# The opening of the first attention: panel splits ahead of late tokens, keys by chunk, and the bias store in another place

## The chip, the core and the metric

One core of one Trainium2 chip runs the kernel. Times are device microseconds of one execution; the kernel before took 1206.1 us as the median of three runs (1205.81 to 1208.53). Its engines are TensorE (PE), VectorE (DVE), ScalarE (ACT), GpSimd (POOL) and SyncE (SP), which here only issues DMA transfers. SP and ACT have a DMA queue each (q1 and q10 in the profile).

## What is computed

A two-layer block (differential attention, then multi-scale pooling, each with a SwiGLU feed-forward) feeds a second block with three sparse attentions and another feed-forward, all in float32 on 256 tokens of width 1024. The change touches the first attention and one store for the second block:

```python
# adaLN: six vectors of 1024 per layer, for the tokens and for the context
m = jax.nn.silu(cond) @ w_mod + b_mod            # split into 6 components
hx = x * (1 + scale) + shift                      # components 0 and 1
hc = context * (1 + c_scale) + c_shift
q = rope(hx @ w_q); k = concat(hc @ w_k, rope(hx @ w_k)); v = concat(hc @ w_v, hx @ w_v)
p = softmax(q_m k_m^T / 8) for m in (0, 1)        # 8 heads, two maps each
o = (p_0 - lam * p_1) v;  o = rms(o) * g;  y = o @ w_o
x = layer_norm(alpha * x + g1 * y)                # g1 is component 2
# second block: 28 relative-bias heads, a row of 384 values each, spread to (28, 128, 384)
```

## The kernel before

**Panels.** All weights pass through a ring of four slots of 1 MB (`ring0` to `ring3`), in the fixed order of `w_panels`. For the attention that is panels 0 to 11: keys of heads 0 to 3 over the first half of the width (0), queries (1), the same keys over the second half (2), queries (3), values of four heads (4, 5), keys of heads 4 to 7 (6, 7), queries (8, 9), values (10, 11). Each panel is split into a high part (`w_hi`, written by ACT, two buffers) and a low part (`ring_lo`, the difference, written by DVE); TensorE computes each product as three matmuls, high x high, high x low, low x high (`product`). ACT may write a high part only when the panel two before is used, SP may load a slot only when the panel four before is used. On ACT and DVE `split_to(i)` writes all parts up to panel i that are still missing, at that place of the engine's own order.

**Tokens.** TensorE turns tokens and context into `whole` by eight chunks of 128 columns. The first four are scaled from PSUM (`high_tokens`, `low_tokens`); the other four wait for the second half of components 0 and 1 and are scaled later. Each of these four raises `late_tokens` by one.

**Components.** Four 2 MB pieces of `w_mod` are multiplied on TensorE (`mod_rows_first`, `mod_columns_first`). The others come in halves m = 0, 1, 2, ... of 2 MB: DVE sums a half in four steps over 1024 columns (`mod_product(m)`), the last step raises `mod_acc`; when both halves of a component are in, TensorE adds over partitions (`mod_sums(comp)`, two banks of the pool "misc", banks 6 and 7) and DVE adds the bias (`mod_finish(comp)`). SP loads half m when `mod_acc` has reached m - 1. Half m has its place in SP's order ahead of a panel: 0 before panel 4, 1 before 5, 2 before 6, 3 before 7, 4 and 5 before 10, 6 before 11, 7 before 12.

**Scores.** Units u = 0 to 7 are four heads by two query tiles. TensorE makes two score maps per unit in the pool "score" (banks 4 to 7: even units 4 and 5, odd units 6 and 7), DVE takes their extrema (`maxima`), ACT the exponentials (`exps`), DVE the mix (`combine`, raises `probs_done`). Between them `maxima_and_mixes` and `scores_out` do panel splits. TensorE then turns the probabilities (pool "misc") and multiplies the values.

**Order.** Every engine runs in program order, and the order of each is written out by hand, in the functions printed below; waits on semaphores alone tie them together. The bias store (`scratch` from `srow`, 28 x 128 rows of 384 values) is issued by ACT at line 1341. SP loads it back as `bias` ahead of panel ("ffn1_in", 6, 1), at line 2682, and waits for `srow_stored` first.

## Time and profile before

| | us |
|---|---|
| median of the runs | 1206.1 |
| the profiled execution | 1208.5 |
| its span, first to last instruction | 1206.7 |
| TensorE busy | 1119.9 |
| DVE busy | 786.0 |
| ACT busy | 491.6 |

The profile is of one execution. A row of a timeline gives the start, the duration, engine, line, operation, the tiles written and read, and in brackets how long the engine had stood idle and what released it. The granted clock is the share of TensorE's full 2.4 GHz; the mean over the span is 0.965. Lines of the kernel stand as L1261. L622 is the one line that issues every matmul, so a matmul is told by its tiles. The shares of the DMA engines are rough near 1.

### The profile page before, as it was taken

Reading aid. Unit: us, or ns where it says so; the run is one execution under the profiler, and the core shown is the slowest. Engines: PE = TensorE matmul, PEld = TensorE weight load, DVE = VectorE, ACT = ScalarE, POOL = GpSimd, SP = SyncE. Lnnn points to the kernel's source line nnn. Section 1 sums busy time; section 2 is a strip of 40 time slices with the busy share of each in tenths; the row PEclk is TensorE's granted clock in tenths of the full one; section 3 lists DMA queues with packets and bytes.
Section 4 is the critical chain, followed back from the end, with each engine's and each line's share of the span. In section 5 each row is a group of like instructions: output and inputs, shape, how many; then the busy total and the mean of one; then the engine's idle time right before and its main releaser. Section 6 shows DMA issues by size and latency. Waiting matters only on the chain.

```text
span 1206.7 us, 17048 instructions
## 1 busy us (share of the span) xinstructions
PE 1119.9 (93%) x7015; PEld 969.1 (80%) x7015; DVE 786.0 (65%) x1073; ACT 491.6 (41%) x625; POOL 99.8 (8%) x84
## 2 busy tenths in 40 slices
PE   4878999979999999599999989999999988999998
PEld 2665786759999877499998878887777767999987
DVE  2376867768878878777554485569873685555543
ACT  2242433534333332433333365465655534434332
POOL 0000000000000001000000000244656000000000
PEclk9788999899999998899999989999999998999999
DMA  9695462483997787257755536534333343555552
GB/s 337 244 378 210 166 253 70 143 310 115 360 330 275 263 300 257 88 172 258 251 175 196 179 115 202 164 116 140 106 116 129 120 159 121 192 177 177 185 198 105
DMA packets 145135, 236.98 MB, mean 196 GB/s; under 512 B 4901, under 2 KB 86306, under 8 KB 144930
## 3 DMA queue, kind: packets, MB, share of 16 engines
q1 hardware_dynamic: 138128, 221.12, 54.1%
q10 hardware_dynamic: 6930, 14.77, 3.3%
q8 instruction: 56, 0.92, 0.3%
q14 instruction: 21, 0.17, 0.0%
HBM read 229.32 MB, written 6.55 MB: 195 GB/s over the span
## 4 chain that ended last, share of the span: by engine, by line
PE 80%; DVE 9%; ACT 4%; issue 4%; DMA 1%; ACTq 1%; POOL 1%; DVEq 0%; SPq 0%
PE bank L622 77%; PE bank L697 3%; ACT w_hi L1261 2%; DVE ring_lo L1661 2%; DMA ring<-in_ffn_w_out 1%; ACTq L1293 1%; DVE modacc L1782 1%; DVE y_tok L1972 1%; DVE small L1974 1%; POOL ring_lo L2604 1%; DVE y_tok L1970 0%; DMA big<-in_ln_b 0%; DVE small L1861 0%; ACT hc_hi L1321 0%; DVE tmp L1845 0%
## 5 line engine op out<-in xcount | busy, mean ns | idle before, releaser
L1661 DVE TENSOR_TENSOR ring_lo<-ring,w_hi 128x2048 fp32r<-128x2048 f32 (+3 forms) x145 | 325.4, 2245 | 274.4 <-ACT w_hi L1261 274.1
L1261 ACT ACTIVATE w_hi<-ring 128x2048 fp32r<-128x2048 f32 (+3 forms) x157 | 295.0, 1880 | 445.9 <-PE bank L622 412.4
L622 PE MATMUL bank<-h_hi,w_hi 128*128 128x256 f32 x1056 | 302.9, 287 | 5.6 <-DVE h_lo L1680 3.3
L622 PE MATMUL bank<-h_lo,w_hi 128*128 128x256 f32 x1056 | 300.6, 285 | 0.0
L622 PE MATMUL bank<-h_hi,ring_lo 128*128 128x256 f32 x1056 | 300.5, 285 | 0.0
L622 PEld LDWEIGHTS bank<-h_hi,w_hi 128*128 128x128 f32 x1056 | 204.6, 194 | 7.4 <-DVE h_lo L1680 3.9
L622 PEld LDWEIGHTS bank<-h_lo,w_hi 128*128 128x128 f32 x1056 | 204.7, 194 | 1.0 <-issue 1.0
L622 PEld LDWEIGHTS bank<-h_hi,ring_lo 128*128 128x128 f32 x1056 | 204.5, 194 | 0.0
L622 PE MATMUL bank<-w_hi,h_hi 128*128 128x512 f32 (+4 forms) x320 | 127.2, 398 | 11.1 <-DVE h_lo L1908 7.8
L622 PE MATMUL bank<-w_hi,h_lo 128*128 128x512 f32 (+4 forms) x320 | 123.7, 387 | 0.0
L622 PE MATMUL bank<-ring_lo,h_hi 128*128 128x512 f32 (+4 forms) x320 | 123.6, 386 | 0.0
L622 PE MATMUL bank<-w_hi,ff_hi 128*128 128x512 f32 x264 | 103.0, 390 | 1.4 <-DVE ring_lo L1661 1.0
L622 PE MATMUL bank<-ring_lo,ff_hi 128*128 128x512 f32 x264 | 102.8, 389 | 0.0
L622 PE MATMUL bank<-w_hi,ff_lo 128*128 128x512 f32 x264 | 102.7, 389 | 0.0
L1782 DVE SCALAR_TENSOR_TENSOR modacc<-aux,cs,modacc 128x1024 f32<-128x1024 f32 x70 | 89.8, 1283 | 1.5
L622 PEld LDWEIGHTS bank<-w_hi,h_hi 128*128 128x128 f32 x320 | 62.0, 194 | 25.0 <-DVE h_lo L1908 8.8
L2614 POOL TENSOR_TENSOR small<-small,neghalf 128x1 f32<-128x1 f32 (+2 forms) x16 | 12.9, 803 | 791.5 <-DVE small L1984 450.8
L622 PEld LDWEIGHTS bank<-w_hi,h_lo 128*128 128x128 f32 x320 | 61.7, 193 | 11.3
L622 PEld LDWEIGHTS bank<-ring_lo,h_hi 128*128 128x128 f32 x320 | 62.1, 194 | 10.0
L2604 POOL TENSOR_TENSOR ring_lo<-ring,w_hi 128x512 fp32r<-128x512 f32 x48 | 61.5, 1313 | 49.2 <-ACT w_hi L1261 49.2
L622 PE MATMUL bank<-big 64*128 64x128 f32 (+5 forms) x274 | 55.8, 448 | 6.0 <-issue 1.6
L622 PEld LDWEIGHTS bank<-w_hi,ff_hi 128*128 128x128 f32 x264 | 49.6, 188 | 13.1 <-issue 3.0
(269 smaller groups left out, 1446.5 us busy)
## 6 DMA issues: line engine op xcount, KB each, us to landing
aux<-in_w_mod SPq DMA_DIRECT2D x24, 2048.0 KB, 10.1
ring<-in_ffn_w_in SPq DMA_DIRECT2D x88, 512.0 KB, 4.9
ring<-in_w_in SPq DMA_DIRECT2D x24, 1024.0 KB, 5.0
ring<-in_ffn_w_out SPq DMA_DIRECT2D x22, 1024.0 KB, 5.3
ring<-in_w_ffn_in SPq DMA_DIRECT2D x44, 512.0 KB, 4.6
ring<-in_attn_w_qkv SPq DMA_DIRECT2D x12, 1024.0 KB, 13.3
ring<-in_w_ffn_out SPq DMA_DIRECT2D x11, 1024.0 KB, 5.0
bias_rows<-srow ACTq DMA_DIRECT2D x1, 5376.0 KB
```

Of the source, the lines that this page charges most:

```text
L622: return nc.tensor.matmul(o, l, r, start=start, stop=stop, **kw)
L697: ins = nc.tensor.transpose(bank[0:src.shape[1], i * P:i * P + src.shape[0]], src, ident[0:src.shape[0], 0:src.shape[0]])
L1261: nc.scalar.activation(panel_part(i, 0), raw_panel(i), ACT.Copy).then_inc(w_hi, 1)
L1293: act.dma_start(dst, src).then_inc(cols_landed, 16)
L1661: V.tensor_tensor(panel_part(i, 1), raw_panel(i), panel_part(i, 0).bitcast(F32), ALU.subtract)\
L1782: ins = V.scalar_tensor_tensor(modacc_raw[:, :], w[:, j, :], c, modacc_raw[:, :], ALU.mult, ALU.add)
L1972: step(V.scalar_tensor_tensor(y, x_tok[:, tt, sl], ALPHA, y, ALU.mult, ALU.add))
L1974: step(V.bn_stats(small[:, 100 + 12 * tt + 6 * nb:106 + 12 * tt + 6 * nb], y))
L2604: ins = nc.gpsimd.tensor_tensor(panel_part(i, 1)[:, c, :], raw_panel(i)[:, c, :], panel_part(i, 0)[:, c, :].bitcast(F32), ALU.subtract)
L2614: nc.gpsimd.tensor_tensor(dst, src, exponent, ALU.pow).then_inc(rstd_done, 1)
```

## The change

Six things move; no instruction is added or taken away.

1. ACT and DVE split panel 0 before the early token chunks, and panel 2 (with panel 1) before the late ones.
2. The keys of panel 2 run chunk by chunk over all four heads (`late_keys`), each chunk behind its own `late_tokens`, instead of head by head.
3. TensorE's `mod_sums(2)` goes from between the value tiles to behind the last scores; `mod_sums(3)` and `mod_sums(4)` go later.
4. DVE's `mod_product(1)` goes from in front of the rotary steps to between units 2 to 5 of the scores, `mod_product(2)` from there to behind them; `mod_product(4)`, `mod_finish(2)` and `mod_finish(4)` go later.
5. DVE's split of panel 5 goes behind both rotary pairs.
6. ACT issues the bias store in the second feed-forward ("ffn1", block 1) instead of behind the late token chunks.

```diff
 # TensorE
-                for c in range(PK):
-                    if h == 0 and kg == 1:
-                        pe.wait_ge(late_tokens, c + 1)
...
+            def late_keys():
+                key = ("qkv", 2, 1)
+                w = panel(key)
+                for c in range(PK):
+                    pe.wait_ge(late_tokens, c + 1)
+                    for h in range(4):
+                        ins = product(psum[where[("K", h)][0]], [x[:, c, h * P:(h + 1) * P] for x in w],
+                                      [x[:, PK + c, :] for x in hcT], False, c == PK - 1)
+                        if c == PK - 1:
+                            fills(ins, ("K", h))
+                release(key, ins, ("K", 3))
...
                 queries(0, 0, late_columns)
-                for j in range(4):
-                    keys(0, 1, j)
+                late_keys()
                 queries(0, 1)
...
-                    if i == 3:
+                    if i == 5:
                         mod_sums(3)
...
-                mod_sums(4)
                 swap_keys(2)
                 swap_keys(3)
                 queries(1, 1)
+                mod_sums(4)
...
-                if hg == 0:
-                    mod_sums(2)
                 vals(hg, 0, 1)
...
                 for u in (6, 7):
                     scores(8 * hg + u)
+                if hg == 0:
+                    mod_sums(2)
 # ACT
+            split_to(0)
             for n in (0, 1):
                 wait_emptied(act, ("modcol", n))
...
-            split_to(1)
+            split_to(2)
...
-            act.wait_ge(srow_done, 1)
-            act.dma_start(scratch, srow[:, :].unsqueeze(1).broadcast_to([REL_HEADS, P, SROW])).then_inc(srow_stored, 16)
...
+                    if name == "ffn1" and nb == 1:
+                        act.wait_ge(srow_done, 1)
+                        act.dma_start(scratch, srow[:, :].unsqueeze(1).broadcast_to([REL_HEADS, P, SROW]))\
+                            .then_inc(srow_stored, 16)
 # DVE
+            split_to(0)
             for ch in range(PK):
                 low_tokens(ch)
...
-            split_to(1)
+            split_to(2)
...
-            def maxima_and_mixes(hg):
+            def maxima_and_mixes(hg, m):
...
                     if 2 <= u <= 5:
-                        mod_product((2, 6)[hg], [u - 2])
+                        mod_product(m, [u - 2])
...
-            split_to(2)
+            split_to(3)
             mod_product(0)
-            split_to(3)
-            mod_product(1)
             split_to(4)
             turn_pair("K", 0)
             turn_pair("K", 1)
-            split_to(5)
             turn_pair("Q", 0)
             turn_pair("Q", 1)
+            split_to(5)
+            maxima_and_mixes(0, 1)
             mod_finish(2)
-            maxima_and_mixes(0)
+            mod_product(2)
             mod_product(3)
             split_to(8)
             mod_finish(3)
-            mod_product(4)
             head_var(0)
             head_norm(0)
+            mod_product(4)
+            split_to(9)
             mod_product(5)
             split_to(10)
-            mod_finish(4)
...
             head_norm(1)
+            mod_finish(4)
...
-            maxima_and_mixes(1)
+            maxima_and_mixes(1, 6)
```

DVE between `mod_product(0)` and the first scores, as the kernel before has it. L1661 is the low part of a panel (the number is its ring slot), L1777 and L1782 are `mod_product`, L1845 to L1849 the rotary steps, L1800 is `mod_finish(2)`, L1861 a `maxima`:

```order
L1777 TENSOR_SCALAR modacc<-aux,cs 128x1024
L1782 SCALAR_TENSOR_TENSOR modacc<-aux,cs,modacc 128x1024 x3
L1661 TENSOR_TENSOR ring_lo3<-ring3,w_hi1 128x2048
L1782 SCALAR_TENSOR_TENSOR modacc<-aux,cs,modacc 128x1024 x4
L1661 TENSOR_TENSOR ring_lo0<-ring0,w_hi0 128x2048
...
L1849 TENSOR_TENSOR big<-big,tmp 128x2x256
L1661 TENSOR_TENSOR ring_lo1<-ring1,w_hi1 128x2048
...
L1800 SCALAR_TENSOR_TENSOR aux<-bank,aux 128x512 x2
L1861 TENSOR_REDUCE small<-bank 128x2 x2
```

And the same stretch now, to the first `mod_product` step between the scores (lines are 12 or 13 higher: L1673 low part, L1858 to L1862 rotary steps, L1794 `mod_product`, L1874 `maxima`):

```order
L1794 SCALAR_TENSOR_TENSOR modacc<-aux,cs,modacc 128x1024 x3
L1673 TENSOR_TENSOR ring_lo0<-ring0,w_hi0 128x2048
L1858 TENSOR_TENSOR tmp<-bank,big 128x512
...
L1862 TENSOR_TENSOR big<-big,tmp 128x512
L1673 TENSOR_TENSOR ring_lo1<-ring1,w_hi1 128x2048
L1874 TENSOR_REDUCE small<-bank 128x2 x2
...
L1887 SCALAR_TENSOR_TENSOR aux<-tmp,small,aux 128x512
L1794 SCALAR_TENSOR_TENSOR modacc<-aux,cs,modacc 128x1024
```

The four L1782 of `mod_product(1)` behind `ring_lo3` have gone down among the scores, one to a unit, and the low part of ring slot 1 stands behind the rotary steps.

SP's order is the same in both kernels; with its waits it reads, from half m2 on:

```order
L480 DMA aux<-in_w_mod 128x4x1024 [waits mod_acc]
L2688 DMA ring2<-in_attn_w_qkv 128x4x512 [waits bank_filled3]
L480 DMA aux<-in_w_mod 128x4x1024 [waits mod_acc]
L2688 DMA ring3<-in_attn_w_qkv 128x4x512 [waits bank_filled5]
L2688 DMA ring0<-in_attn_w_qkv 128x4x512 [waits w_used]
```

These are m2, panel 6, m3, panel 7 and panel 8. Nothing moved, but the second `mod_acc` wait is now for sums that DVE makes among the scores.

TensorE at the end of the scores of units 6 and 7, before (`big` are the scores, `hc_hi,w_hi0` the keys of panel 6) and now:

```order
L622 MATMUL bank<-big 128x512 x4
L622 MATMUL bank<-hc_hi,w_hi0 128x512
```

```order
L622 MATMUL bank<-big 128x512 x4
L622 MATMUL bank<-modacc,ones 128x512 x2
L622 MATMUL bank<-hc_hi,w_hi0 128x512
```

The two matmuls of `mod_sums(2)` stand between the last scores and the next keys.

## Rows read from the trace of the kernel before

**Rows 1.** The page of the kernel before, part 1: busy time of each engine.

```profile
PE 1119.9 (93%) x7015; PEld 969.1 (80%) x7015; DVE 786.0 (65%) x1073; ACT 491.6 (41%) x625; POOL 99.8 (8%) x84
```

**Rows 2.** Timeline of TensorE: start us, us, engine, line, op, tiles, xcount, [idle before].

```profile
38.14 0.77 PE L622 MATMUL bank<-hc_hi,w_hi 128*128 128x512 f32 x1 [3.07 <-DVE ring_lo L1661]
...
69.91 0.77 PE L622 MATMUL bank<-hc_hi,w_hi 128*128 128x512 f32 x1 [6.67 <-DVE ring_lo L1661]
...
97.25 1.10 PE L622 MATMUL bank<-modacc,ones 128*128 128x512 f32 x2 [2.09 <-DVE tmp L1845]
99.28 1.22 PE L622 MATMUL bank<-modacc,ones 128*128 128x512 f32 x1 [0.93 <-DVE tmp L1845]
...
130.15 1.99 PE L622 MATMUL bank<-big 64*128 64x512 f32 x8
...
137.64 1.03 PE L697 MATMUL bank<-table,aux 128*128 128x128 f32 x8
```

**Rows 3.** One stretch: us, PE busy, granted clock, DMA share, GB/s.

```profile
98.00:105.00 7.00, 6.07 (x13) 0.53 0.85 325
```

**Rows 4.** Timeline of DVE: last late chunk, low part 2, end of mod_product(2).

```profile
66.91 0.69 DVE L1833 TENSOR_TENSOR hc_lo<-big,hc_hi 128x512 fp32r<-128x512 f32 x1
67.52 2.29 DVE L1661 TENSOR_TENSOR ring_lo<-ring,w_hi 128x2048 fp32r<-128x2048 f32 x1
...
129.81 1.28 DVE L1782 SCALAR_TENSOR_TENSOR modacc<-aux,cs,modacc 128x1024 f32<-128x1024 f32 x1
```

**Rows 5.** Timeline of ACT: two key copies, w_hi of panels 6 and 7.

```profile
75.08 0.60 ACT L1344 ACTIVATE big<-bank 128x512 f32<-128x512 f32 x1 [6.74 <-PE bank L622]
77.82 0.60 ACT L1344 ACTIVATE big<-bank 128x512 f32<-128x512 f32 x1 [2.15 <-PE bank L622]
...
113.61 1.91 ACT L1261 ACTIVATE w_hi<-ring 128x2048 fp32r<-128x2048 f32 x1 [2.39 <-PE bank L622]
...
134.02 1.92 ACT L1261 ACTIVATE w_hi<-ring 128x2048 fp32r<-128x2048 f32 x1
```

**Rows 6.** DMA issues at 9.8 and 217 us: KB each, us to landing.

```profile
ring<-in_attn_w_qkv SPq DMA_DIRECT2D x1, 1024.0 KB, 16.7
...
aux<-in_w_mod SPq DMA_DIRECT2D x1, 2048.0 KB, 7.8
ring<-in_attn_w_o SPq DMA_DIRECT2D x1, 1024.0 KB, 10.4
```

**Rows 7.** Timeline of SP's queue: m3, and panel 7 with the two behind it.

```profile
83.67 1.41 SPq L480 DMA_DIRECT2D aux<-in_w_mod  x1
89.01 41.61 SPq L2675 DMA_DIRECT2D ring<-in_attn_w_qkv  x3
```

**Rows 8.** DMA queues, 60.9 to 105.5: packets, MB, share of 16 engines.

```profile
q1 hardware_dynamic: 3806, 10.94, 64.6%
q10 hardware_dynamic: 3593, 5.50, 32.9%
```

**Rows 9.** Two stretches, second feed-forward: busy by engine, clock, DMA share, GB/s.

```profile
535.50:562.80 27.30, 27.30 (x230) 27.30 (x230) 25.25 (x22) 9.65 (x7) 0.00 (x0) 1.00 0.65 219
562.80:584.00 21.20, 21.20 (x169) 20.24 (x168) 9.86 (x9) 7.23 (x6) 0.00 (x0) 1.00 1.07 342
```

**Rows 10.** Timeline of SP's queue: bias load, and the panel issues behind it.

```profile
562.82 0.43 SPq L2682 DMA_DIRECT2D aux<-bias_rows  x1
567.54 6.80 SPq L2675 DMA_DIRECT2D ring<-in_ffn_w_in  x2
```

**Rows 11.** Timeline of ACT, second feed-forward: splits and one issue of rows.

```profile
532.99 1.91 ACT L1261 ACTIVATE w_hi<-ring 128x2048 fp32r<-128x2048 f32 x1 [3.85 <-PE bank L622]
...
544.51 0.39 ACTq L1279 DMA_DIRECT2D aux<-in_ln_g  x1
...
581.99 1.91 ACT L1261 ACTIVATE w_hi<-ring 128x2048 fp32r<-128x2048 f32 x1 [5.06 <-DMA ring<-in_ffn_w_in]
...
586.53 1.92 ACT L1261 ACTIVATE w_hi<-ring 128x2048 fp32r<-128x2048 f32 x1 [2.14 <-PE bank L622]
```
## The prediction

> **What bounds the kernel now.** The page comes first: TensorE is busy 93% of the span [rows 1], so only what shortens or lengthens TensorE's own path counts. Its rows in order of time show where it stands still in the first attention: 3.07 us before the first key product, 6.67 us before the second key panel, until DVE has written that panel's low part, and 2.09 and 0.93 us at the sums of component 2, which wait for DVE's rotary steps [rows 2]. After such a pause the granted clock sits at half, the 1.2 GHz level: 0.53 as a mean from 98 to 105 [rows 3]. The first key tile of the second panel took from 69.91 to its copy at 75.08, 5.2 us, the next one 2.74 us [rows 2, 5]; so the pause of 6.67 us cost 2.4 us more. Then I read the queues behind the moved steps: DVE, ACT, SP, and the two DMA queues, here and in the second feed-forward, where the bias store goes.
>
> Panels are numbered by their place in the loading order: 0 and 2 are the first four key heads, 4 and 5 the values, 6 and 7 the other keys; m0 to m3 are the first 2 MB halves of w_mod.
>
> **Step 1, splits ahead of the tokens.** ACT's w_hi of panel 0 (1.9 us a panel) moves ahead of the four early token chunks. The panel is there: issued at 9.85, it took 16.7 us and landed at 26.6 [rows 6], about when ACT begins those chunks. The token chain slides 2 us, and the last transposes, which ended at 38.14 - 3.07 = 35.1, end at 37.1. Before, TensorE had to wait beyond them for the low part; now that is long done. The first product comes at 37.1 and not 38.14; at half clock about half of it stays: **0.6 us gained**. Panel 2 is now split before the late tokens. Its w_hi waits only until panel 0 is used, and its low part (2.29 us, rows 4) ends about 55.7 instead of standing in front of TensorE. The copies of the two w_mod sums now queue behind it on DVE, until 57.1; TensorE asks for them at 57.8, so that wait is hidden by 0.7 us.
>
> **Step 2, keys chunk by chunk.** The last late chunk is done at 67.5 [rows 4]; with the shift of 0.6 the four come at 62.8, 64.2, 65.6 and 66.9. One chunk for four heads is 12 products, 2.74 us. So TensorE waits for the first chunk alone, about 0.2 us, and never again: **6.5 us gained**, and with the clock kept **2.2 us**. The fourth key tile is full at 73.8, not 83.1, a lead of 9.3 us.
>
> **Step 3, the sums of component 2.** They leave their place between the value tiles. There they cost 2.09 + 0.93 us of waits and 1.10 us each, 5.2 us [rows 2], and the slow clock behind them, 6 us of products at half speed, 3.0 us [rows 3]. DVE now turns keys and queries with no low part between them and is ahead of TensorE. The lead when panel 4 is released and ACT begins panel 6 (113.61 before, rows 5) is 9.3 + 5.2 + 3.0, some **17.7 us**: 95.9.
>
> **Step 4, what this starts to wait for.** mod_product(1) moves in between the softmax steps, where mod_product(2) stood. Its last step, which ended there at 131.1 [rows 4], ends at 131.1 - 17.7 + 0.5 = 113.9 (a multiply-add of 1.28 us in the first place instead of 0.75). SP may issue m3 only when that sum is counted, and **panel 7 is queued behind m3 on SP**. Before, the two went out at 83.67 and 89.01 [rows 7]; now both at 114.0. A pair of the same sizes, issued 0.4 us apart, landed after 7.8 and 10.4 us [rows 6], so panel 7 lands at 124.8. ACT has its split between the last two exponentials (134.02 before, rows 5); it would come there at 116.4 and stands until 124.8. exps(7) follows at 126.7. TensorE is through with the scores (130.15 + 1.9 before) at 114.0 and now meets the sums of component 2, whose banks 6 and 7 are those of the last scores: exps(7) frees them at 127.4 and 128.1. TensorE idles 13.4 us, starts at 1.2 GHz, and the next keys begin at 129.2. With about 3 us of them slow, the probabilities of units 0 and 1 are turned at 136.4, against 137.64 [rows 2]. Of 17.7 us **1.2 stay**.
>
> **Step 5, the rest of the attention.** mod_sums(3) and (4) are the same instructions later; DVE does mod_finish, mod_product(4) and low part 9 in a new order. DVE then reaches the second rotary pair 2.3 us later, which the wait for low part 11 covers; query tile 3 is full 1.7 us earlier, but the value tile behind it needs TensorE as long as before. I count **0.4 us gained** (0 to 1.5). Opening in all: **-1.6 us**, between -4 (the clock recovers early, twice) and +0.5 (panel 7 lands 2 us later).
>
> **Step 6, the bias store in the second feed-forward.** The store takes 32.9% of the 16 DMA engines for 44.6 us, **14.7 us of all of them** [rows 8]. At its old place TensorE did not wait for the loads that it slowed. ACT now issues it right behind the split at 532.99 [rows 11]; its 0.93 us of issue are covered by ACT's idle time. From 535.5 to 562.8 the engines are 0.65 busy, and 1.07 is what they reach when full [rows 9]: 27.3 x 0.42 = 11.5 us are free. The store needs 14.7. At 562.82 SP wants to issue the load of the bias, which waits for the store, and the next panel is behind it [rows 10]. So SP stands for the last 3.2 us of the store, a share of the panel in flight and the landing, some 2 to 6 us; I take 4. That next panel was already the tightest: it went out at 567.54 behind the load, ACT waited 5.06 us for it until 581.99, and its two splits (1.9 and 2.3 us) ended at 586.2, where TensorE changed panels at about 586.5, as the next split shows [rows 10, 11]. So 0.3 us is left. A delay of 4 is a pause of 3.7 us on TensorE and, as above, some 2.4 us of slow clock: **+6.1 us**.
>
> There is a second way to the same price. ACT issues the normalisation rows at 544.51, now behind the store [rows 11]. On SP the issues behind the big bias load were held: 6.80 us for two [rows 10]. If ACT is held in the same way until the store is two thirds done, about 554.5, its next split starts at 555.6 instead of 550.3, the low part is ready at 559.9, and TensorE, which changes panels at 556.0, pauses 3.9 us: 6.3 with the clock. SP's delay is then absorbed, since TensorE comes later. The cost is **6 us by either way, 12 if both add up, 0 if neither holds**.
>
> The Trainium skill (DMA: Bandwidth & Descriptors, Queues, rings and completion order) says that each DMA engine takes turns between its queues packet by packet, so a store from ACT does not stand behind SP's panels but between them. In the stretch of the old store the rows agree: 3806 packets of one queue, 3593 of the other [rows 8]. By that rule alone each panel beside the store would land some 4 us later, within the two panels that it has, and the sum would stay as above.
>
> **Sum.** -1.6 + 6.0 = +4.4 us. The profiled execution had a span of 1206.7 us and a time of 1208.5, 2.4 above the median of 1206.1; on its own terms it becomes a span of 1211.1. Against the median I say **1210.5 us**.
>
> **Rivals.**
> A (forecast, 0.50): panel 7's late load swallows the opening's lead, and the store costs 3 to 8 us: 1207.5 to 1213.
> B (0.27), not slower: the store fits. The deciding point is 562.8: if the engines can give it 0.54 of those 27.3 us, nothing waits. For it: the engines reached 1.07 with other packets, and larger ones may run quicker. Against it: the free share as read is 0.42. Then only -1.6 is left, 1204.5, down to 1202 with the better end of the opening.
> C (0.10), clearly faster: the lead survives, because something I hold for fixed is not, such as panel 7 landing within 3 us of the sum, or TensorE having work across the wait. With 1.3 us of new waits and the store free, 1206.1 - 17.7 + 1.3 = 1189.7; with step 6, 1195.7. Against it: the pair in rows 6 took 10.4 us.
> D (0.13), worse: both ways of step 6 add up, or panel 7 lands late as well: +10, 1216.
>
> **How the numbers follow.** The measurement tells about 0.3%, 3.6 us. Slower by more than that: 0.38 of A's 0.50 and all of D, 0.51. Within it: 0.12 of A and 0.19 of B, 0.31. Faster: 0.08 of B and all of C, 0.18. The range may leave out 0.2: 1201.5 to 1216 leaves C and the far part of D.
>
> **What the new profile would show.** Right: the first product near 37, the second key panel near 63 with no pause; m3 and panel 7 issued together near 114; ACT waiting about 8 us for a ring landing, and TensorE pausing 13 us ahead of the component 2 sums; in the second feed-forward a bias load that SP issues several us late against its panel, or an ACT issue of the normalisation rows that takes many us, and a TensorE pause of 3 to 5 us with a half-clock stretch behind it. Wrong: the first probabilities turned before 130 (step 4), or a bias load that did not wait for the store (step 6).

## The result, and the profile after

| | before | after |
|---|---|---|
| median, us | 1205.95 (4 runs, 1204.85 to 1208.53) | 1215.37 (4 runs, 1214.24 to 1216.12) |
| ratio, 95% interval | | 1.0078 [1.0064, 1.0092] |
| span of the profiled execution | 1206.7 | 1213.9 |

The change makes the kernel 9.4 us slower; 1210.5 was predicted, in a range of 1201.5 to 1216. The direction and the first cause (the opening's gain is mostly swallowed by a late panel 7) came out as forecast. The store in the second feed-forward cost more than twice its term.

**The opening.** TensorE of after, in order of time (to compare with [rows 2]):

```profile
60.78 0.47 PE L622 MATMUL bank<-hc_hi,w_hi 128*128 128x512 f32 x1 [0.27 <-DVE hc_lo L1846]
...
111.32 1.99 PE L622 MATMUL bank<-big 64*128 64x512 f32 x8
125.57 2.04 PE L622 MATMUL bank<-modacc,ones 128*128 128x512 f32 x2 [12.26 <-ACT big L1374]
...
134.39 1.03 PE L697 MATMUL bank<-table,aux 128*128 128x128 f32 x8
```

The pause of 6.67 us before the second key panel is 0.27 us. The last scores are issued at 111.3 and not 130.2: 18.8 us ahead. Then TensorE stands 12.26 us in front of the sums of component 2, and of the lead 3.25 us is left when the first probabilities are turned (134.39 against 137.64). The chain behind that pause can be read backwards through ACT, DVE and SP:

```profile
113.85 0.69 ACT L1374 ACTIVATE big<-bank,small 128x512 f32<-128x512 f32 x1 [1.44 <-DVE small L1874]
...
122.85 1.91 ACT L1271 ACTIVATE w_hi<-ring 128x2048 fp32r<-128x2048 f32 x1 [7.55 <-DMA ring<-in_attn_w_qkv]
124.67 0.67 ACT L1374 ACTIVATE big<-bank,small 128x512 f32<-128x512 f32 x1
```

```profile
110.99 1.28 DVE L1794 SCALAR_TENSOR_TENSOR modacc<-aux,cs,modacc 128x1024 f32<-128x1024 f32 x1
```

```profile
112.29 0.37 SPq L480 DMA_DIRECT2D aux<-in_w_mod  x1
112.70 3.88 SPq L2688 DMA_DIRECT2D ring<-in_attn_w_qkv  x3
```

The last step of mod_product(1) on DVE ends at 112.27, SP issues m3 at 112.29 and panel 7 at 112.70. ACT is through with the exponentials of unit 6 at 115.3 and stands 7.55 us for panel 7, whose split lies ahead of the exponentials of unit 7. Those free the banks 6 and 7 that TensorE wants. Before, SP had both loads out by 89.0 [rows 7].

**The second feed-forward.** ACT's rows of after, to set beside [rows 11]:

```profile
528.70 1.91 ACT L1271 ACTIVATE w_hi<-ring 128x2048 fp32r<-128x2048 f32 x1 [3.85 <-PE bank L622]
528.71 0.93 ACTq L1473 DMA_DIRECT2D bias_rows<-srow  x1
...
540.22 1.92 ACT L1271 ACTIVATE w_hi<-ring 128x2048 fp32r<-128x2048 f32 x1 [3.84 <-PE bank L622]
540.23 13.51 ACTq L1289 DMA_DIRECT2D aux<-in_ln_g  x1
553.78 2.04 ACTq L1289 DMA_DIRECT2D aux<-in_ln_b  x1
555.92 0.60 ACT L1480 ACTIVATE tmp<-bank 128x512 f32<-128x512 f32 x1 [13.78 <-issue]
556.41 1.90 ACT L1271 ACTIVATE w_hi<-ring 128x2048 fp32r<-128x2048 f32 x1
```

An issue that took 0.39 us takes 13.51 us, with the store ahead of it in the same queue. ACT does nothing meanwhile ("13.78 <-issue"), and TensorE, out of split panels, stops:

```profile
563.28 0.55 PE L622 MATMUL bank<-h_hi,w_hi 128*128 128x256 f32 x1 [11.58 <-DVE ring_lo L1673]
```

Behind it 96 products take 14.26 us instead of 11.6, at half clock. The pause and the slow clock together are 14.2 us. The DMA engines in windows of after (columns as in [rows 9]):

```profile
540.00:550.00 10.00, 10.00 (x86) 10.00 (x85) 3.69 (x3) 1.92 (x1) 0.00 (x0) 1.00 0.96 271
550.00:560.00 10.00, 1.70 (x15) 1.50 (x13) 3.35 (x5) 2.44 (x3) 0.00 (x0) 0.77 1.01 297
560.00:570.00 10.00, 6.72 (x35) 6.75 (x36) 9.54 (x8) 2.35 (x2) 0.00 (x0) 0.55 0.93 295
```

They are full at 271 to 297 GB/s, while [rows 9] shows 342 GB/s when they are full of panels and the bias load. So two suspects stood in this stretch: ACT's held issue, and panels that land late beside the store. The experiments had to part them.

**Where the time stands, place by place.** ACT's split of a panel starts when TensorE has used the panel two before it, so the same split in two traces gives the lead or lag of the whole program. In us against before, negative is ahead; ordinary numbers are differences of two rows of ACT's timelines. The profiled execution of the kernel before (1208.53 us) is its slowest of the four, 2.6 us above the median, so a lead in this table can be that much too large:

| split at (before) | after | store back | m3 later | both | sums 2nd key |
|---|---|---|---|---|---|
| 64.6 (panel 2) | -15.4 | -15.4 | -15.6 | -17.9 | -15.7 |
| 113.6 (panel 6) | -19.4 | -19.4 | -19.5 | -21.9 | -19.7 |
| 147.4 (panel 8) | -3.2 | -3.0 | -11.0 | -12.9 | -16.6 |
| 267.9 | -4.7 | -4.4 | -12.2 | -13.9 | -15.8 |
| 538.8 | -4.3 | -3.9 | -12.6 | -13.3 | -15.2 |
| 567.6 | +10.0 | -3.9 | +0.7 | -13.3 | -15.2 |
| 975.0 | +9.9 | -4.0 | +1.6 | -13.0 | -15.1 |
| 1126.3 | +7.2 | -5.3 | +3.2 | -14.4 | -16.4 |

The columns are the kernel after and four of the experiments below. Between 975 and 1126 nothing differs in the code; some 1 to 3 us there, and the 2 us by which "both" is early at its first panels (its first keys had the full clock), are differences between single executions.

### The profile page after: what moved, and what is told of

The parts are those of the page before. It is cut to its first block, busy times and chain, and to the rows that moved or that the text cites. A ratio compares the mean times of both kernels' runs of the same rounds, so it can differ in the third digit from the quotient of the medians.

```text
span 1213.9 us, 17049 instructions
## 1 busy us (share of the span) xinstructions
PE 1112.8 (92%) x7015; PEld 964.8 (79%) x7015; DVE 785.9 (65%) x1073; ACT 491.9 (41%) x625; POOL 101.8 (8%) x84
## 4 chain that ended last, share of the span: by engine, by line
PE 76%; DVE 10%; ACT 4%; issue 4%; DMA 2%; ACTq 1%; POOL 1%; SPq 1%; DVEq 0%
PE bank L622 74%; PE bank L697 2%; DMA ring<-in_attn_w_qkv 2%; ACT w_hi L1271 2%; DVE ring_lo L1673 2%; ACTq L1289 1%; DVE modacc L1794 1%; DVE y_tok L1985 1%; DVE small L1987 1%; DVE y_tok L1983 1%; POOL small L2627 1%; DVE small L1874 1%; SPq L2671 1%; POOL ring_lo L2617 1%; ACT hc_hi L1331 0%
## 5 line engine op out<-in xcount | busy, mean ns | idle before, releaser
L1673 DVE TENSOR_TENSOR ring_lo<-ring,w_hi 128x2048 fp32r<-128x2048 f32 (+3 forms) x145 | 325.4, 2244 | 284.4 <-ACT w_hi L1271 284.1
L622 PE MATMUL bank<-h_hi,w_hi 128*128 128x256 f32 x1056 | 303.7, 288 | 17.4 <-DVE ring_lo L1673 11.6
L622 PEld LDWEIGHTS bank<-h_hi,w_hi 128*128 128x128 f32 x1056 | 205.4, 194 | 19.5 <-issue 13.0
L622 PE MATMUL bank<-w_hi,h_hi 128*128 128x512 f32 (+4 forms) x320 | 127.0, 397 | 10.7 <-DVE h_lo L1921 7.8
L1794 DVE SCALAR_TENSOR_TENSOR modacc<-aux,cs,modacc 128x1024 f32<-128x1024 f32 x70 | 89.7, 1282 | 1.6
```

What stands on the lines that cost most here:

```text
L622: return nc.tensor.matmul(o, l, r, start=start, stop=stop, **kw)
L1673: V.tensor_tensor(panel_part(i, 1), raw_panel(i), panel_part(i, 0).bitcast(F32), ALU.subtract)\
L1794: ins = V.scalar_tensor_tensor(modacc_raw[:, :], w[:, j, :], c, modacc_raw[:, :], ALU.mult, ALU.add)
```

## Experiments

Each ratio is to the kernel before on the same chip. There the kernel before scattered over some 9 us (1200.1 to 1209.7), so a difference of medians below 2 us says little; traces decide such points.

**1. The store back at its old place.** The kernel after with

```diff
+            act.wait_ge(srow_done, 1)
+            act.dma_start(scratch, srow[:, :].unsqueeze(1).broadcast_to([REL_HEADS, P, SROW])).then_inc(srow_stored, 16)
             def key_copy(h):
...
-                    if name == "ffn1" and nb == 1:
-                        act.wait_ge(srow_done, 1)
-                        act.dma_start(scratch, srow[:, :].unsqueeze(1).broadcast_to([REL_HEADS, P, SROW]))\
-                            .then_inc(srow_stored, 16)
```

> The kernel after with the bias store issued again behind the late token chunks. Theory (the store's new place costs the second feed-forward some 14 us, the opening has gained 4 to 5.6 us that last to its start): the pause of 11.6 us in the second feed-forward is gone, the lead of 4.3 us at its second split stays to the end, time about 1201.5 us. Rival 1 (part of the opening's gain came from the store being out of the opening, 14.7 us of all engines' time from 61 to 105): the second key panel, the sums or panel 6 come later, time 1203 to 1207. Rival 2 (my forecast: opening -1.6, store +6): time 1204.5.

1203.82 us, ratio 0.9985 [0.9966, 1.0004]. The lead at 538.8 us, 3.9, is still 4.0 at 975 (the table). The opening's steps up to panel 6 come as early as in after to 0.1 us, so the old place of the store held nothing up and its removal gave nothing there: rival 1 is out by its sign, though the time lies in its range (and near rival 2's) and not at the theory's 1201.5. The opening alone is worth 2 to 4 us.

**2. The store alone moved.** The kernel before with step 6 of the change only.

```diff
-            act.wait_ge(srow_done, 1)
-            act.dma_start(scratch, srow[:, :].unsqueeze(1).broadcast_to([REL_HEADS, P, SROW])).then_inc(srow_stored, 16)
...
+                    if name == "ffn1" and nb == 1:
+                        act.wait_ge(srow_done, 1)
+                        act.dma_start(scratch, srow[:, :].unsqueeze(1).broadcast_to([REL_HEADS, P, SROW]))\
+                            .then_inc(srow_stored, 16)
```

> The kernel before with only the bias store moved to block 1 of the second feed-forward. Theory (ACT's issue of ln_g stands behind the store for some 13 us, as in the trace of after): ACT's issue takes 13 us, TensorE pauses 11 to 12 us near 556 to 568, time about 1206 + 14 = 1220 us. Rival 1 (my forecast for that edit): +6, 1212. Rival 2 (taking the store out of the opening gives something back there): the opening ends earlier than before, first probabilities turned before 137 us, time 1216 to 1218.

1220.73 us, ratio 1.0115 [1.007, 1.0159]. ACT and TensorE repeat the rows of after:

```profile
543.67 13.73 ACTq L1279 DMA_DIRECT2D aux<-in_ln_g  x1
...
566.92 0.55 PE L622 MATMUL bank<-h_hi,w_hi 128*128 128x256 f32 x1 [11.77 <-DVE ring_lo L1662]
```

So step 6 costs 14 us by itself, whatever the opening does (the interval allows 8 to 19; in the trace the lead at ACT's splits falls by 14.3 us).

**3. m3 behind panels 7 to 9.** The kernel after, SP's order alone changed; the store stays in the second feed-forward.

```diff
-            halves_before = {RING: [0], 5: [1], 6: [2], 7: [3], 10: [4, 5],
+            halves_before = {RING: [0], 5: [1], 6: [2], 10: [3, 4, 5],
...
```

> The kernel after with the w_mod half m3 loaded behind panels 7, 8 and 9 instead of ahead of them (SP alone changes). Theory (panel 7's landing, held behind m3 that waits for the sum of half 1, is what ACT and then TensorE wait for): panel 7 is issued near 85 to 95 us, ACT's wait of 7.55 us for its landing and TensorE's idle 12.3 us ahead of the component 2 sums are gone or below 2 us, the first probabilities are turned at 118 to 122 us instead of 134.4, and, if nothing later gives it back, the time is 1215.4 - 14 = 1201 us. Rival 1 (the pause stands for DVE's mix or the banks 6 and 7, not for the panel): the pause stays above 6 us, time above 1209. Rival 2 (the lead is lost later, to components whose halves now land later, or to value and query panels not yet there): opening as in the theory, but the lead at 252 us is below 10 us, time 1206 to 1212.

1211.98 us, ratio 1.0049 [1.0027, 1.007]. TensorE at the sums of component 2:

```profile
117.72 1.08 PE L622 MATMUL bank<-modacc,ones 128*128 128x512 f32 x1 [4.60 <-ACT big L1374]
```

The idle time falls from 12.26 to 4.60 us and ACT no longer waits for a landing. The lead at panel 8 is 11.0 us instead of 3.2, and it holds until 538.8 (12.6). Then the store takes 13.3 us of it. So the cause of the pause was the place of m3. My number for what stays, below 2 us, missed the other part: the split of panel 7 and the exponentials of unit 7 are done one after the other between the scores and the sums, 4.6 us in any case. The time is 11 us above the theory's 1201, where I had counted 14 us for what was 7.7; the first probabilities are turned at 126.7, not at 118 to 122. Its ratio lies 0.0029 (3.5 us) below that of after, with uncertainties of 1.7 and 2.6 us. The two traces are 8.3 us apart at 975 us, but 4.1 us at 1126 and 4.0 in their spans. So the traces of the opening show the cause, and how much of the time of after it is stays open between some 4 and 8 us (from experiment 1 to 5, the same edit, it is 6 us by the ratios).

**4. The normalisation rows issued later.** The kernel after with `ln_load(3)` in block 5.

```diff
-                    if name == "ffn1" and nb == 2:
+                    if name == "ffn1" and nb == 5:
                         ln_load(3)
```

> The kernel after with the two loads of the normalisation rows issued by ACT in block 5 of the second feed-forward instead of block 2; the store stays in block 1. Theory (it is ACT's own issue, held behind the store, that stops the splits): no ACT issue above 2 us before block 5, the TensorE pause of 11.6 us near 552 is gone; what is left is SP's wait for the store ahead of the bias load, until some 565 us, and a pause of 0 to 4 us with up to 2.4 us of slow clock behind it: 1202 to 1208 us. Rival 1 (the store's traffic delays the panels, whatever ACT does): ACT waits for a ring landing instead, the pause stays above 8 us, time above 1212.

1214.14 us (1210.61 to 1217.60), ratio 1.0076 [1.0053, 1.01], which is the ratio of after; the theory's 1202 to 1208 missed. The profiled execution is the fastest of the eight. In it no issue of ACT is held, and what the held issue had covered comes into view on ACT:

```profile
551.88 1.91 ACT L1271 ACTIVATE w_hi<-ring 128x2048 fp32r<-128x2048 f32 x1 [8.72 <-DMA ring<-in_ffn_w_in]
560.56 1.92 ACT L1271 ACTIVATE w_hi<-ring 128x2048 fp32r<-128x2048 f32 x1 [6.77 <-DMA ring<-in_ffn_w_in]
```

TensorE pauses 4.02, 1.22 and 2.03 us there. So both mechanisms are real and lie over each other; take one away and most of the price stays: all but 1 us of it by the medians, 8.6 of 14.2 us in this fastest execution (3.8 us ahead at the split of 538.8, 4.8 behind at 975). The edit also takes the 1 MB of the two loads out of the stretch, so what the hold alone is worth is not separated from them. The wait of SP for the store, the first way of my step 6, is next to nothing:

```profile
SPq L2695 <- DMA bias_rows<-srow: 1.1, 1, 1.1
```

and the two queues from 530 to 560 (packets, MB, share of 16 engines) show why the panels are late:

```profile
q10 hardware_dynamic: 3100, 4.76, 58.3%
q1 hardware_dynamic: 3427, 3.41, 37.2%
```

In 30 us the panels get 3.4 MB, a packet of 1 KB for each of the store's. In the kernel before they got 5.7 MB in the same window:

```profile
q1 hardware_dynamic: 5722, 5.68, 58.5%
```

Half a panel (0.5 MB) takes 13.6 us to land from 528 to 568, against 4.9 before:

```profile
ring<-in_ffn_w_in SPq DMA_DIRECT2D x12, 512.0 KB, 13.6
```

**5. Both edits**, 1 and 3 together.

> The kernel after with both edits: the store back behind the late token chunks, and m3 behind panels 7 to 9. Theory (the two losses are independent): the lead is 12.1 us at 147 us, as with m3 moved alone, and is still there at the end, as the lead with the store moved back alone was: time 1206.1 - 12.1 = 1194.0 us. Rival (the store's traffic from 66 to 100 us now meets the earlier panels 7, 8 and 9): the lead is below 9 us, time above 1197.

1196.18 us, ratio 0.9935 [0.9912, 0.9958]: the lead of the opening (12.9 at panel 8) reaches the end. The two losses are independent. The time is 2.2 us above the theory's 1194.0 and still below the rival's 1197.

**6. The sums behind the first key product** of panel 6, on top of both.

```diff
                 for u in (6, 7):
                     scores(8 * hg + u)
-                if hg == 0:
-                    mod_sums(2)
...
                     keys(1, i // 4, i % 4)
+                    if i == 0:
+                        mod_sums(2)
```

> As the one with both edits, and the sums of component 2 behind the first key product of panel 6 instead of ahead of it. Theory (the 4.6 us that TensorE still waits with m3 moved is for exps(7), which frees the banks of the sums, and the 5.74 us key product covers it): the pause is below 1 us, with 0.7 us of slow clock saved: 5 us faster than with both edits, 1189 us. Rival (the pause moves on to the first turned probabilities or values, which wait for the mix on DVE): pause of 3 us or more at another place, below 2 us faster.

1194.23 us, ratio 0.9916 [0.9884, 0.9948].

```profile
118.14 1.10 PE L622 MATMUL bank<-modacc,ones 128*128 128x512 f32 x2 [1.66 <-ACT big L1377]
```

The pause of 4.60 falls to 1.66, not below 1: the key product ran at full clock and took 3.0 us, since it is 12 products and not the 24 that I had counted. From the second key panel to panel 8 it gains 4.9 us on the kernel with both edits, of which 3.2 are left at panel 9. By the medians it gains 2.0 us and misses the theory's 1189.

**7. The splits behind the tokens**, on top of both: panels 0 and 2 are split where the kernel before does it; the keys stay chunk by chunk.

```diff
 # ACT and DVE alike
-            split_to(0)
...
-            split_to(2)
+            split_to(1)
```

> As the one with both edits, and the splits of panels 0 and 2 behind the token chunks again, where the kernel before has them; the keys stay chunk by chunk. Theory (the low part of panel 2 is what the pause of 6.67 us stood for; without it early, the chunk order gives nothing): first product at 38.1 us, pause of 5 to 7 us before the second key panel and slow clock behind it: 9 to 11 us slower than with both edits, if nothing later hides it. Rival (the wait was for the late chunks themselves): pause below 2 us, within 4 us of both edits.

1206.89 us, ratio 1.0028 [1.0008, 1.0048].

```profile
37.53 0.77 PE L622 MATMUL bank<-hc_hi,w_hi 128*128 128x512 f32 x1 [3.07 <-DVE ring_lo L1671]
...
68.04 0.77 PE L622 MATMUL bank<-hc_hi,w_hi 128*128 128x512 f32 x1 [6.68 <-DVE ring_lo L1671]
```

Both pauses of [rows 2] are back, of the same size, and the time is 10.7 us longer: the theory. This run says something of step 3 of my prediction, too. Its lead is 10.6 us at the split of panel 6 and 0.7 at panel 8 ("both" goes from 21.9 to 12.9). Behind the last scores, the sums of component 2 and the pause of 4.60 us thus stand in a stretch that grew by 9 to 10 us, about as much as leaving the old place had saved (8.2 by step 3). What is left of the opening comes mostly from the splits and the chunk order.

**8. The keys by head**, on top of both: `keys(0, 1, j)` behind all four chunks; the splits stay ahead.

```diff
-                late_keys()
+                for c in range(PK):
+                    pe.wait_ge(late_tokens, c + 1)
+                for j in range(4):
+                    keys(0, 1, j)
```

> As the one with both edits, and the second half of the keys head by head, behind all four late chunks, as in the kernel before; the splits stay ahead. Theory: the fourth late chunk comes 3 x 1.4 = 4.2 us behind the first one, so TensorE waits 4.2 us at the second key panel instead of 0.3, and half of 4 us of clock is lost behind it: 4 to 7 us slower than with both edits. Rival (the splits alone carry the gain): within 2 us of both edits.

1203.32 us, ratio 0.9999 [0.9981, 1.0018].

```profile
66.04 0.77 PE L622 MATMUL bank<-hc_hi,w_hi 128*128 128x512 f32 x1 [4.70 <-DVE hc_lo L1848]
```

A pause of 4.70, near the 4.2 worked out, and 7.1 us longer. Each alone leaves most of the 6.67 us standing, 4.70 with the splits and 6.68 with the chunk order. A kernel with neither and both other edits was not run, so what each is worth by itself is open.

**9. Half of the rows in the second feed-forward.** m3 later; rows 0 to 13 are stored at the old place, rows 14 to 27 in block 1.

```diff
+            def store_rows(lo, hi):
+                act.dma_start(scratch[lo:hi], srow[lo:hi, :].unsqueeze(1).broadcast_to([hi - lo, P, SROW]))\
+                    .then_inc(srow_stored, 16)
...
+            store_rows(0, REL_HEADS // 2)
...
+                        store_rows(REL_HEADS // 2, REL_HEADS)
```

> m3 behind panels 7 to 9, and the bias store in two: rows 0 to 13 behind the late token chunks, rows 14 to 27 in block 1 of the second feed-forward, with the normalisation rows in block 2. Between the kernel with the whole store there (1212.0 us) and the one with none there (1196.2 us). Theory (ACT's issue is held only while a long queue of the store's packets is ahead of it; it was let go 25 of 36 us into the whole store, so about a third of its packets, 1200, may wait; half a store has 1792, of which 11.5 us later some 650 are left): ln_g's issue takes below 2 us, the engines are full for some 18 us instead of 36, TensorE's pause is 0 to 2 us, time 1196 to 1199. Rival (any store there costs a fixed amount, by ACT's issue or by SP's wait): pause above 5 us, time above 1203.

1220.12 us, ratio 1.0134 [1.0099, 1.0168]: half of the bytes cost more than all of them, 8 us above the kernel with the whole store there (1211.98). ln_g's issue is not held (0.33 us; ln_b's 3.75), as the theory said, but its time is far off. The rival's pause and time came true, and its reason, a fixed price, did not, as 12 shows. ACT waits 9.07 and 13.18 us for landings and TensorE pauses 3.89 and 9.60 us:

```profile
567.61 0.55 PE L622 MATMUL bank<-h_hi,w_hi 128*128 128x256 f32 x1 [9.60 <-DVE ring_lo L1678]
```

The queues from 530 to 560, as under 4:

```profile
q10 hardware_dynamic: 1713, 2.78, 68.3%
q1 hardware_dynamic: 2273, 2.27, 22.7%
```

Half as many packets of the store's queue hold the engines for longer (the normalisation rows are among them): 68.3% of 480 us by 1713 is 191 ns a packet, against 90 ns under 4 (58.3% by 3100). At the old place the other half does harm too, which the whole store did not: panel 6 lands late (ACT waits 5.13 us), panel 7 is split 7 us later than in 3. By the splits of ACT, 8 us of the lead are gone before the second feed-forward (4.5 us are left at 538.8, 12.6 in 3). In the second feed-forward this half then costs 18.4 us up to the split of 567.6, and the whole store cost 13.3 there.

**10. mod_product(1) early.** The store back; mod_product(1) ahead of the split of panel 4, so that m3 can keep its place ahead of panel 7.

```diff
             mod_product(0)
+            mod_product(1)
             split_to(4)
...
-            maxima_and_mixes(0, 1)
+            maxima_and_mixes(0, None)
```

> The kernel after with the store back behind the late token chunks, and mod_product(1) ahead of the rotary steps and of the split of panel 4; m3 stays ahead of panel 7 on SP, and the softmax steps have no sum between them. Theory (m3, and panel 7 behind it, waited for that sum alone): m3 is issued near 77 us, panel 7 lands before 100, ACT's wait of 7.7 us and TensorE's idle 12.4 us shrink to 4.6 as with m3 moved; the split of panel 4 on DVE ends 3 us later, so TensorE waits 0.5 to 3 us there: 1196 to 1200 us. Rival (the wait for panel 7 has another cause): idle above 9 us, time 1203.8 or more.

1196.06 us, ratio 0.9923 [0.9898, 0.9947]. The rows of SP's queue:

```profile
76.83 0.37 SPq L480 DMA_DIRECT2D aux<-in_w_mod  x1
77.32 33.23 SPq L2688 DMA_DIRECT2D ring<-in_attn_w_qkv  x3
```

m3 is issued at 76.83, panels 7 to 9 from 77.32 on, and TensorE's idle time at the sums is 4.61 us, as with m3 moved. TensorE waits less than 0.5 us for the split of panel 4. So the pause of after had one cause, m3 behind the late sum and panel 7 behind m3, and can be undone at either end.

**11. The sums behind the second key product**, otherwise as 6.

```diff
                     keys(1, i // 4, i % 4)
+                    if i == 1:
+                        mod_sums(2)
```

> Store back, m3 behind panels 7 to 9, and the sums of component 2 behind the second key product of panel 6. Behind the first key product 1.66 us of wait were left. Theory: they go, 1 to 2 us faster than that (1194.2 us), 1193. Rival (the first turned probabilities then wait for the banks of the sums, which DVE empties after its mixes): a pause of 2 us or more behind the sums, 1194 to 1197.

1192.36 us, ratio 0.9897 [0.9871, 0.9924]: the lowest time here, 1.0% below the kernel before (the interval overlaps that of 6). The pause at the sums is gone, and the lead at panel 8 is 16.6 us, 15.0 in 6. A pause stands in front of the first turned probabilities, as the rival has it, but it is small:

```profile
120.91 1.23 PE L697 MATMUL bank<-table,aux 128*128 128x128 f32 x8 [0.59 <-DVE aux L1811]
```

**12. Half of the copies in the second feed-forward.** The same bytes and packets as in 9, cut the other way: 64 of the 128 copies of all 28 rows.

```diff
+            def store_copies(lo, hi):
+                act.dma_start(scratch[:, lo:hi, :], srow[:, :].unsqueeze(1).broadcast_to([REL_HEADS, hi - lo, SROW]))\
+                    .then_inc(srow_stored, 16)
...
+            store_copies(0, P // 2)
...
+                        store_copies(P // 2, P)
```

> As the kernel with the store in two halves, but cut the other way: all 28 rows, 64 of the 128 copies each time, the first half behind the late token chunks, the second in block 1 of the second feed-forward. Bytes and packets of each half are the same as there; the rows come out of 28 partitions instead of 14. Theory (a store's speed goes by the partitions that it reads, and a packet of it costs the engine the more, the fewer they are: 96 ns each with 28 rows, 192 ns with 14): the half in the second feed-forward lasts about 18 us instead of 36, ln_g's issue is not held, panels 6 and 7 are split as early as with m3 moved alone, TensorE's pauses in the second feed-forward sum to 0 to 4 us, time 1196 to 1202. Rival 1 (a store in two costs twice, whatever its cut): as with 14 rows, 1220. Rival 2 (any traffic of ACT's queue there stops the panels for as long as it lasts, the whole store's price by half): 1204.

1204.25 us, ratio 0.9979 [0.9965, 0.9993]: 16 us better than the same bytes out of 14 partitions. Panels 6 and 7 are split as early as in 3 (19.6 and 19.1 us ahead), so theory and trace agree for the old place. In the second feed-forward the theory's pauses of 0 to 4 us and its time (1196 to 1202) missed, and the time is rival 2's. ACT and TensorE:

```profile
546.61 1.91 ACT L1271 ACTIVATE w_hi<-ring 128x2048 fp32r<-128x2048 f32 x1 [9.94 <-DMA ring<-in_ffn_w_in]
```

```profile
550.99 0.55 PE L622 MATMUL bank<-h_hi,w_hi 128*128 128x256 f32 x1 [6.07 <-DVE ring_lo L1678]
```

The lead falls from 11.1 us (split of 538.8) to 2.8 (567.6). So half the store there costs 8.3 us of lead where the whole one cost 13.3, about 0.6 of the price; by the ratios (0.9979 between 0.9935 and 1.0049) it is 0.4. ln_g's issue plays no part in the pause (0.40 us), so late panels alone can make one.

## Why the prediction was right or wrong

Two slips in the working are small: the terms of step 3 add up to 17.5, not 17.7, and in step 4 TensorE would be through with the scores at 114.4, not 114.0.

**Step 1, splits ahead.** The mechanism holds (experiment 7). I gave it 0.6 us, with a first product at 37.1; it came near 36.5 and the 48 products behind it ended at 49.2 instead of 51.9, 2.7 us gained. The clock came back sooner than "half of it stays" assumed.

**Step 2, keys by chunk.** Second key panel at 60.78 with 0.27 us of wait, forecast 62.9 and 0.2. The lead at the fourth key tile is 11.3 us (split of panel 4 at 71.97 against 83.26), forecast 9.3; the 2 us are step 1's.

**Step 3.** w_hi of panel 6 at 94.26, a lead of 19.4; forecast 17.7. Right in its size, with the same 2 us. That the new place of the sums costs about what the old one did, even without a late panel (experiment 7), I had not seen; the late panel covered it.

**Step 4.** Each link was as written, with sizes close: the sum counted at 112.3 (forecast 113.9), both loads behind it, landing 10.1 us after the issue (10.8), ACT's wait 7.55 (8), TensorE's pause 12.26 (13.4), first probabilities at 134.4 (136.4). 3.25 us stayed instead of 1.2. Experiments 3 and 10 showed the cause from both ends.

**Step 5.** 0.4 us forecast, 1.4 found (3.25 at the probabilities, 4.7 at 268 us). The opening was worth -4.7 in the trace where I had -1.6; the steps before it made 2.0 of the difference, this one 1.0. The better end that I gave, -4, was too tight.

**Step 6 failed in its size: +14.2 instead of +6.** Four links of it, one by one:

1. "27.3 x 0.42 = 11.5 us are free. The store needs 14.7." The 14.7 came from [rows 8], 65 ns a packet of the store between panel packets of 3 KB. In the feed-forward it took 90 ns, 20 us of all engines. And room between bursts is not what a panel sees: it is needed back soon, and while a store runs, it gets packets one for one.
2. "By that rule alone each panel beside the store would land some 4 us later, within the two panels that it has, and the sum would stay as above." This was the sentence with which I set contention aside. The rule itself (the Trainium skill, DMA: Bandwidth & Descriptors, Queues, rings and completion order) agrees with the packet counts above, 3427 to 3100. But one for one, 1 KB against 1.5 KB of the slower kind, leaves the panels 3.4 MB in 30 us where they had 5.7, and half panels land after 13.6 us instead of 4.9. Experiments 4 and 12 show pauses from that alone.
3. "So SP stands for the last 3.2 us of the store, a share of the panel in flight and the landing, some 2 to 6 us": 1.1 us in experiment 4, none in after, where TensorE is late first. The "first way" was the wrong one.
4. "If ACT is held in the same way until the store is two thirds done, about 554.5": it was held until 553.7. That ACT is held was right. The close hit on the time was luck: the store was issued 4.3 us earlier than in the kernel before, and the hold ended 25 us behind it instead of 21.5. Its price was wrong, 11.6 us of pause for 3.9. TensorE ran dry at 551.7 and not at 556.0, since the lead was 4.3 us; 556.0 is the time of the kernel before, so I had carried no lead at all into this step, not even my own 1.6 us. And the low part was ready at 563.1, not 559.9: behind ACT's issue stood a second one (2.04), the SiLU, and on DVE the mix of the block and two multiply-adds of a w_mod half ahead of the low part.

"6 us by either way, 12 if both add up, 0 if neither holds": the first way took no part. Beside the second stood the late panels that I had set aside, and the two lay over each other. The verdict, slower by more than 0.3%, had 0.51. The time is 4.9 us above the forecast; it lies 0.6 us inside the range, above rival A's own 1207.5 to 1213 and next to rival D's 1216. That it is inside owes something to luck, two errors of opposite sign: the opening 3 us better than said, the store 8 us worse.

## What to carry to other kernels

A moved load or store takes its queue with it: list what is issued behind it on that engine, by size and due time, both where it was and where it goes. A semaphore that a sum raises is part of that list: the later sum here cost 8 us through a load in front of a panel, and moving that load behind three panels gave it back. And do not cost a transfer by its bytes or by its share of busy time at another place. Ask out of how many partitions it comes, at what pace it will run there, and how late the loads beside it will land.

## What the hardware showed

**A store has a fast start and then a pace, which is lower out of fewer partitions.** From 88 us on the store of experiment 1 is alone on the engines. Its queue from 88 to 90, then from 90 to 96, and that second window of the core (columns as in [rows 9]):

```profile
q10 hardware_dynamic: 379, 0.58, 91.0%
```

```profile
q10 hardware_dynamic: 668, 1.03, 86.5%
```

```profile
90.00:96.00 6.00, 6.00 (x27) 3.87 (x25) 3.09 (x5) 4.53 (x9) 0.00 (x0) 1.00 0.87 171
```

That is 290 GB/s at 77 ns of an engine for each packet, and then 171 GB/s at 124 ns, with nothing beside it either time. In experiment 4 it starts in the same way beside packets of 1 KB: 65 ns from 534 to 536, 310 GB/s from 536 to 538, and then, from 538 to 564, 166 GB/s:

```profile
q10 hardware_dynamic: 2814, 4.32, 65.2%
```

So a packet's time on an engine is not fixed, and at its pace the store holds the engines for longer while it moves less. At its old place it ran below that pace, at 123 GB/s as a mean and one for one with packets of 3 KB, and took 65 ns a packet [rows 8].

Out of 14 partitions instead of 28 the pace is lower. In experiment 9 from 534 to 544 it is 95 GB/s, at 191 ns a packet, so half the packets lasted about as long as all:

```profile
q10 hardware_dynamic: 620, 0.95, 74.0%
```

At the old place the packets of 28 partitions took 65 ns each (experiment 12: 14.3% of 51 us for 1806 packets), those of 14 took 137 ns (30.3%). The Trainium skill (SBUF — State Buffer, Door 1: The DMA port swizzle) says that the rate goes by the ports which the partitions reach. By its map 28 partitions from 0 reach 7 ports and partitions 14 to 27 reach 4; at its 27.2 GB/s a port that is an estimate of 190 and 109 GB/s. The two paces lie 10 to 13% below, and their ratio, 0.56 to 0.57, is nearer to 4 of 7 ports than to 14 of 28 partitions. But the start at 290 to 310 GB/s lies far above 190, so ports alone do not account for the store, and what ends its fast start is not shown. Runs with 14 rows on more ports, which would tell ports from partitions, were not tried.

**A queue holds its issuer.** Behind the whole store of 3584 packets, issued 11.5 us earlier, ACT's issue of ln_g took 13.5 to 13.7 us (after, experiments 2 and 3). Behind half as many packets it took 0.33 and 0.40 us, and the next one, ln_b, 3.75 and 2.09 us (experiments 9 and 12). The three long holds ended with 2478, 2503 and 2518 of the 3584 packets through, so with some 1070 to 1110 left; in 9 and 12, 847 and 663 were left when ln_g was issued. For this first issue the limit in these runs thus lies between 847 and about 1100 packets. ln_b, right behind it, waited 2 to 3.75 us with as many or fewer left; it does not fit that number, and its cause is open.

**What a pause costs in clock.** After 11.6 us of pause the granted clock was 0.55 over ten us (window 560 to 570) and 2.7 us were added; after 4.02 us in experiment 4 the next 48 products took 7.5 instead of 5.8 us.
